# Six buffers for gathered expert rows instead of four, and rows asked for two to three blocks ahead

## The reference

```python
q = (xb @ w_pq).reshape(TOK_BLOCK, PEER_HEADS, 2, D_KEY_HALF)
s = jnp.einsum('thcd,hcnd->thcn', q, sub_keys)
s1, i1 = lax.top_k(s[:, :, 0], PEER_TOPK)       # 16 of 128 keys, for each half
s2, i2 = lax.top_k(s[:, :, 1], PEER_TOPK)
...
top_s, pos = lax.top_k(cand_s, PEER_TOPK)       # 16 of 256 pairs
eidx = jnp.take_along_axis(cand_i, pos, axis=-1)
g = jax.nn.softmax(top_s, axis=-1)
u = jnp.take(u_exp, eidx, axis=0)
a = jax.nn.gelu(jnp.einsum('thkd,td->thk', u, xb))
w = (g * a).astype(xb.dtype)
return jnp.einsum('thk,thkd->td', w, jnp.take(v_exp, eidx, axis=0))
```

## Time and profile before

| what | value |
|---|---|
| median of 3 runs | 4145.35 us (4144.81 to 4147.48) |
| the profiled execution | 4145.56 us |
| its span | 4143.8 us |
| TensorE busy | 3886.4 us (94%) |
| DVE busy | 2826.8 us (68%) |
| ACT busy | 1696.9 us (41%) |
| POOL busy | 2232.5 us (54%) |
| HBM read and written | 969.3 MB, 234 GB/s |

### The profile page before, as it was taken

One profiled execution on the slowest core, in us unless ns is written; L12 is line 12 of the kernel. 1 busy time (PEld: TensorE's weight loads), 2 busy tenths in 40 slices (PEclk: granted clock), 3 DMA queues, 4 the chain that ended last, 5 costly groups with the idle time before them and its releaser, 6 DMA issues.

```text
span 4143.8 us, 57586 instructions
## 1 busy us (share of the span) xinstructions
PE 3886.4 (94%) x21170; PEld 3362.8 (81%) x21170; DVE 2826.8 (68%) x4491; ACT 1696.9 (41%) x2936; POOL 2232.5 (54%) x1240
## 2 busy tenths in 40 slices
PE   7978899999999999999979989999999999999997
PEld 5756898888888888878769989888888888788876
DVE  3774227988875588888863322788887548888886
ACT  3264324556666322222231132455666632222223
POOL 1101234665556677777742323465565667777774
PEclk9999999999999999999999999999999999999998
DMA  5302224778888998898945312477888889988994
GB/s 201 124 1 110 100 99 164 249 269 284 292 299 309 314 307 303 301 314 297 316 147 182 107 57 92 160 243 258 280 300 282 311 312 306 314 295 299 313 316 160
DMA packets 395800, 972.44 MB, mean 235 GB/s; under 512 B 32048, under 2 KB 221232, under 8 KB 381744
## 3 DMA queue, kind: packets, MB, share of 16 engines
q1 hardware_dynamic: 301664, 630.72, 45.2%
q0 software_dynamic: 92160, 335.59, 22.7%
q10 hardware_dynamic: 1744, 3.21, 0.2%
HBM read 835.37 MB, written 133.96 MB: 234 GB/s over the span
## 4 chain that ended last, share of the span: by engine, by line
issue 41%; POOL 34%; PE 17%; DMA 4%; DVE 3%; ACT 1%; POOLq 0%; DVEq 0%; ACTq 0%
POOL SL L444 18%; POOL ROWS L451 14%; PE PS L762 10%; PE PS L564 5%; POOL SL L435 3%; DMA ROWS<-u_exp,EI 2%; DMA ROWS<-v_exp,EI 1%; PE PS L754 1%; DVE ROWS L1267 1%; PE PS L715 1%; DVE OH L1256 0%; DVE PO L1193 0%; ACT SH L995 0%; PE PS L774 0%; DVE TS L1188 0%
## 5 line engine op out<-in xcount | busy, mean ns | idle before, releaser
L444 POOL TENSOR_TENSOR SL<-RW,SH 128x1024 fp32r<-128x1024 f32 x512 | 1284.0, 2508 | 928.6 <-ACT SH L995 887.7
L774 PE MATMUL PS<-WH,SH 128*128 128x480 f32 x2048 | 786.9, 384 | 63.3 <-DVE WL L1317 60.7
L762 PE MATMUL PS<-HH,SH 128*128 128x480 f32 x2048 | 804.5, 393 | 7.8 <-POOL SL L444 6.5
L995 ACT CAST SH<-RW 128x1024 fp32r<-128x1024 f32 x512 | 535.9, 1047 | 613.8 <-PE PS L762 514.1
L762 PE MATMUL PS<-HL,SH 128*128 128x480 f32 x2048 | 780.0, 381 | 0.0
L762 PE MATMUL PS<-HH,SL 128*128 128x480 f32 x2048 | 779.8, 381 | 0.0
L774 PE MATMUL PS<-WH,SL 128*128 128x480 f32 x2048 | 777.2, 379 | 0.0
L774 PE MATMUL PS<-WL,SH 128*128 128x480 f32 x2048 | 776.9, 379 | 0.0
L435 POOL TENSOR_TENSOR SL<-RW,SH 128x1024 fp32r<-128x1024 f32 x84 | 202.5, 2414 | 815.8 <-ACT SH L819 815.8
L1034 ACT CAST WH<-GL 128x480 fp32r<-128x480 f32 x256 | 152.0, 594 | 938.1 <-DVE GL L1311 934.0
L1273 DVE SCALAR_TENSOR_TENSOR ACC<-ROWS,AA,ACC 128x1024 f32<-128x1024 f32 x256 | 399.1, 1559 | 186.8 <-DMA ROWS<-v_exp,EI 174.4
(11 more groups left out here) (171 smaller groups left out, 5358.6 us busy)
## 6 DMA issues: line engine op xcount, KB each, us to landing
RW<-u_blk SPq DMA_DIRECT2D x256, 512.0 KB, 4.3
RW<-v_blk SPq DMA_DIRECT2D x256, 512.0 KB, 5.5
gate_acts<-GE SPq DMA_DIRECT2D x256, 240.0 KB, 2.9
router_weights<-GT SPq DMA_DIRECT2D x60, 1024.0 KB, 4.7
GB<-router_weights SPq DMA_DIRECT2D x32, 1920.0 KB, 12.7
GL<-gate_acts SPq DMA_DIRECT2D x256, 240.0 KB, 4.7
RW<-wstream SPq DMA_DIRECT2D x100, 512.0 KB, 4.5
AW<-wpairs SPq DMA_DIRECT2D x40, 1024.0 KB, 5.2
```

Source lines behind the costliest of these rows:

```text
L444: nc.gpsimd.tensor_tensor(SL[:, r % 2], RW[:, r % RAW], SH[:, r % 2].bitcast(F32), ALU.subtract).then_inc(raw_used, 1)
L762: last = mm(PS[:, n % 2, NG:NS], w[:, n % 2, j], a[:, j, NG:NS], start=(j == 0 and q == 0), stop=(j == DJ - 1 and q == 2))
L774: last = mm(PS[:, dj, NG:NS], w[:, k % 2, dj], a[:, k, NG:NS], start=start, stop=stop)
L995: nc.scalar.copy(SH[:, r % 2], RW[:, r % RAW]).then_inc(hi_done, 1)
```

## The change

RING goes from 4 to 6. ROWS becomes a list of six buffers, the first four where they were, the other two in the space SK. In its turn n POOL now asks for the rows that DVE uses in block n + 2 of the u stage. In the v stage it asks for those of block n + 3, and in turn 0 for all those up to block 3. The uses on DVE name the buffers in the new way and stay where they are.

```diff
-RING = 4
+RING = 6
...
-    ROWS, _ = sb("ROWS", [P, RING, D], F32, at=at_BIG)
+    ROWS = [sb(f"ROWS{k}", [P, D], F32, at=at_BIG + k * D * 4 if k < 4 else at_SK + (k - 4) * D * 4)[0]
+            for k in range(RING)]
...
                 pool.wait_ge(row_used, n + 1)
                 pool.sem_inc(rows_asked)
                 nc.gpsimd.indirect_dma_start(
-                    ROWS[:, n % RING], None, table[l],
+                    ROWS[n % RING][:], None, table[l],
                     bass.IndirectOffsetOnAxis(ap=EI[:, c:c + 1], axis=0)).then_inc(row_in[n % RING], 16)
...
             for n in range(NB_E):
                 low(n + 1)
                 for s in range(NPICK):
-                    if PICK_AT[s] == n + 1:
+                    if PICK_AT[s] == n + 2:
...
             for n in range(NB_E):
                 low(NB_E + n + 1)
                 for s in range(NPICK):
-                    if VPICK_AT[s] == n + 1:
+                    if max(VPICK_AT[s], 3) == n + 3:
                         gather(v_exp, 1, s)
...
-                v.tensor_tensor_reduce(ROWS[:, n % RING], ROWS[:, n % RING], HTOK[:] if s < PG else HTOK_PS,
+                v.tensor_tensor_reduce(ROWS[n % RING][:], ROWS[n % RING][:], HTOK[:] if s < PG else HTOK_PS,
...
-                v.scalar_tensor_tensor(acc[:], ROWS[:, n % RING], AA[:, c:c + 1], acc[:],
+                v.scalar_tensor_tensor(acc[:], ROWS[n % RING][:], AA[:, c:c + 1], acc[:],
```

## The result

| | before | with the change |
|---|---|---|
| median | 4145.97 us (4144.81 to 4147.48, 4 runs) | 4003.61 us (3999.92 to 4008.57, 4 runs) |
| the profiled execution | 4145.56 us | 3999.92 us |
| its span | 4143.8 us | 3998.1 us |

The ratio is 0.9658, with a 95% interval of 0.9644 to 0.9671: 142 us less. The forecast was 4027 us, so the direction and the places were right, and the gain was 23 us larger than the sum.

What follows compares the result with a forecast made beforehand. DVE's waits for gathered rows were taken to hold up TensorE in the dense stages; 4145.4 - 78.6 (v) - 40 (u) = 4026.8 us, with DMA and buffers priced at 0; range 3996 to 4090 us.

Steps and rivals of the forecast that it cites:

- What bounds the kernel: Dense u and v stages: DVE, stretched by waits for gathered rows (322.2 us u, 219.0 us v), is what TensorE waits for.
- The v stage: Rows asked three turns ahead end DVE's row waits; TensorE sets the pace at 5.25 us a block, 78.6 us saved.
- The strict sum of all operations by the exclusive port: v block: each DVE operation and each SL one behind the other, 5.44 us a block, only 30 us saved.
- The u stage: Rows asked two turns ahead; two thirds of 60.6 us of one-hot stalls and slow clock go, 40 us saved.
- The clock: Half-clock stretches right after eight u-stage stalls cost 18.7 us; dips in both stages would be mostly gone.
- The DMA rival: DMA is full: weights come late at 316 GB/s, v saves 53 us, u 30, 4062 us; chance 0.15.
- The port rival: Shared port replaces the rows: DVE's v block becomes 5.44 us, WL late again, 4075 to 4095 us; chance 0.17.
- The slower rival: POOL holds SL back for a used buffer, 5.2 us a hold; 30 holds give 4183 us; chance 0.04.
- What would show it: Signs: v row waits under 20 us, WL waits under 20, v stages about 672, clock dips mostly gone, GL mean up.

Runs made afterwards that it cites:

- the run with the second WL: Against the whole change: one more DVE operation before each WL in the v blocks, GL - WH written to an unused place; 4112.69 us, ratio 0.9924.
- the run with the sum: Against the whole change: one more DVE operation per v block, a sum over GL's 480 columns with one SBUF input; 4076.51 us, ratio 0.9832.

## Why the prediction was right, and where it was short

**What bounds the kernel: right.** DVE's row waits were what TensorE waited for, by way of WL and of the one-hots. Without them TensorE waits for neither. That the waits are caused by the time of asking and not by a lack of room is shown by the first two runs, one with the buffers alone (nothing) and one with the asks alone (nearly all).

**The v stage: right, 78.6 us forecast, 86.6 measured.** The step "a DVE block with its SL takes 5.03 us, under TensorE's 5.20" held: DVE is busy for 4.95 us a block, and the run with the second WL gives 5.08 for it. The 0.05 us that I added a block for seams was not there; 5.21 and 5.22 were measured. The strict sum of all operations by the exclusive port, 5.44 us and 30 us saved, would have been wrong by over 50 us. The rule of the Trainium skill's page "SBUF — State Buffer", section "Who interferes with whom", is seen in the 2.66 us of a WL that meets SL. A block's length does not follow from adding all recorded spans up, though the 0.4 us that I called overlap of the two engines is not all that. Recorded spans of neighbours on DVE overlap each other as well: in the earlier trace rows WL stands for 0.65 us and GL starts 0.57 us behind it, and in the same profile the row of 1.29 us at 1722.80 is followed by WL at 1724.00. How much of the 0.4 us is left for the port is not shown.

**The u stage: the step that was mis-sized.** I counted 41.9 us of stalls behind the one-hots and 18.7 us of half clock, 60.6 us, and then took two thirds of it, 40 us. 59.8 us were measured: the count was right and the discount was not. The parts fit too: in the windows of the two u stages TensorE's idle time fell by 35.5 us and its busy time, in which the slow clock lies, by 24.3. I had justified it with blocks where DVE would be at its limit from routing, one-hots and rows. Only 3.9 us of waits behind the one-hots are left there, of the 37.7 in the earlier trace rows. Between 720 and 1180 us DVE is busy for 412.2 us, 90% of TensorE's 459.6, as forecast. But it is ahead now: in this stretch it waits 38.2 us for TensorE before its one-hots, where it was 3.5 us, as these lines of before and of after show:

```profile
DVE OH L1256 <- PE PS L754: 3.5, 6, 1.1
```

```profile
DVE OH L1257 <- PE PS L755: 38.2, 25, 4.4
```

An engine that is ahead can take a heavy stretch without anybody waiting. The work of a stretch had been measured in the earlier trace rows; the time that DVE gains before it was what I left out. In the profiled executions the forecast is 27 us short: this term makes up 20 of them, and the v stages 8. The medians, 23 us short, have some 3 us of scatter beside it.

**The clock: right.** The dips in both stages were tied to the stalls and went with them, those in the u stages with the early u rows alone.

**The DMA rival: not met.** The v stages move 317 GB/s at a share of 0.91, as worked out, and TensorE does not wait.

**The port rival: near.** It is not what happened, but the run with the second WL shows that 0.57 us more of DVE work per block would have made DVE the bound.

**The slower rival: the price was wrong.** I had 5.2 us for each hold of POOL at a full ring. With three buffers 463 us of holds cost 128 us, 0.28 us for each us and 0.7 us for each hold. SL has slack: the 135 us of holds in the u stages cost some 5 us, and the 328 us in the v stages cost 123. With six buffers holds before SL came to 13.3 us. The reason that I gave against this rival was right for six buffers, which need the row of the block before POOL's turn. It does not cover four, which need the row of the turn's own block: at the ask of 1706.22 in the earlier trace rows that row's use only came at 1706.67. That four are enough comes from the change itself, which makes DVE use its rows earlier.

**What would show it: one sign was wrong.** I wrote that the mean of the GL product would rise. It fell, and that of WL rose. The seam above suggests why: ACT, no longer held by DVE, rounds SH when TensorE lets it and WH right behind it, so SL starts just before WL can. This is not the whole rule: with v rows two turns ahead the means in the first v stage are 1044 ns for GL, 1094 for WL and 2132 for the row uses on ACC, so there it is the row uses that meet SL, and the stage is as short.

## What to carry to other kernels

When an engine waits for gathered data, look at how long before its use it is asked for, and against the landing time, before buying buffers: here one turn more in each stage was worth 3.3%, and two buffers more 0.2% if anything. A ring's need for room has to be judged with the consumer's timing after the change, not with the late one that the profile shows. Count stalls with the slow clock behind them, and do not discount such a count unless a row shows that something else is late at the same places.

## What the runs showed of the hardware that I had not expected

- A DVE operation whose start is recorded first does not always win the shared port, or the recorded start is not the moment at which the port is taken; the trace does not tell which. The GL product of the profile before that starts at 1708.44 lasts 3.27 us beside an SL that POOL starts at 1708.79 and ends at 1711.19, though it takes 0.65 us alone:

```profile
1708.44 3.27 DVE L1311 TENSOR_TENSOR GL<-GL,GB 128x480 f32<-128x480 f32 x1
```

```profile
1708.79 2.40 POOL L444 TENSOR_TENSOR SL<-RW,SH 128x1024 fp32r<-128x1024 f32 x1
```

- The wait goes the other way as well. In the run with the sum, an SL that starts inside a pair of row uses, and ends inside the WL behind them, takes 3.35 us instead of 2.39.

```profile
1649.44 2.67 DVE L1275 SCALAR_TENSOR_TENSOR ACC<-ROWS,AA,ACC 128x1024 f32<-128x1024 f32 x2
```

```profile
1651.01 3.35 POOL L446 TENSOR_TENSOR SL<-RW,SH 128x1024 fp32r<-128x1024 f32 x1 [1.41 <-ACT SH L997]
```

- A ring that is too short can cost far less than the time that the issuing engine stands: with three buffers 0.28 us for each us, 0.37 in the v stages.
